# One step of a hybrid attention and state-space encoder on one Trainium2 core: the scan's gate interleaved with the prompt's attention, operand splits moved, preparation reordered

## The reference, cut to what matters

```python
h = rmsnorm(x, g_pre) * (1 + scale) + shift          # shift, scale, gate = split(c @ w_ada + b_ada)
z = h @ w_in                                         # 2048 -> 5712 columns: q, k, v, iq, ik, iw, za, u, zs
# attention group: indexer scores, top-k keys, grouped-query softmax (8 heads, 2 kv heads, 128 wide)
attn = dsa(q, k, v, iq, ik, iw) * silu(za)
# state-space group: 64 groups x 16 channels, 64 complex states each
y = gelu(s5_scan(u))                                 # 1024 columns
y = y * sigmoid(y @ w_glu + b_glu) * silu(zs)        # "the scan's gate"
out = concat([attn, y]) @ w_out                      # 2048 -> 2048
return x + gate * rmsnorm(out, g_post)               # and k, v, ik, last states as outputs
```

## Time and profile before

| | us |
|---|---|
| median of 3 runs | 2370.98 (2365.38 to 2373.74) |
| the profiled execution | 2373.1 |
| its span, first to last instruction | 2371.3 |
| PE busy | 2140.8 (90%) |
| DVE busy | 1268.0 (53%) |
| ACT busy | 718.9 (30%) |
| POOL busy | 355.6 (15%) |
| mean granted clock of TensorE | 0.94 |

### The profile page before, as it was taken

The page is one execution under the profiler, slowest core; times in us unless marked ns, Lnnn a source line. Parts: engine busy times, 40 slices in busy tenths (PEclk is TensorE's granted clock), DMA queues, the critical chain, the costliest instruction groups (busy, mean ns, idle before and its releaser), DMA issues. The chain is left out here.

```text
span 2371.3 us, 33581 instructions
## 1 busy us (share of the span) xinstructions
PE 2140.8 (90%) x12705; PEld 1885.5 (80%) x12705; DVE 1268.0 (53%) x2487; ACT 718.9 (30%) x1433; POOL 355.6 (15%) x614
## 2 busy tenths in 40 slices
PE   5889788899999999999999994978995799998896
PEld 4669788788899999999999994965773578776774
DVE  5446745444324888888776662658764231124224
ACT  5331122211134333333332212336651213321331
POOL 0253652545400000000000000001101100004001
PEclk9999899999999999999999996988997599998997
DMA  9746356555443333333333316232202132227436
GB/s 351 278 164 119 104 127 149 172 172 176 132 117 85 93 95 93 88 93 98 94 90 102 93 52 198 84 117 58 54 1 73 55 90 77 74 71 215 105 93 177
DMA packets 338086, 277.44 MB, mean 117 GB/s; under 512 B 107481, under 2 KB 277409, under 8 KB 336649
## 3 DMA queue, kind: packets, MB, share of 16 engines
q1 hardware_dynamic: 296210, 235.36, 36.1%
q10 hardware_dynamic: 40256, 35.77, 5.0%
q0 software_dynamic: 1472, 4.33, 0.6%
HBM read 215.18 MB, written 60.20 MB: 116 GB/s over the span
## 5 line engine op out<-in xcount | busy, mean ns | idle before, releaser
L1282 PE MATMUL ps_z<-h_hi,w_hi 128*128 128x384 f32 (+2 forms) x1936 | 666.2, 344 | 4.7 <-DVE w_lo L866 4.7
L1284 PE MATMUL ps_z<-h_hi,w_lo 128*128 128x384 f32 (+2 forms) x1936 | 656.9, 339 | 0.0
L1283 PE MATMUL ps_z<-h_lo,w_hi 128*128 128x384 f32 (+2 forms) x1936 | 656.7, 339 | 0.0
L1282 PEld LDWEIGHTS ps_z<-h_hi,w_hi 128*128 128x128 f32 (+1 forms) x1936 | 362.8, 187 | 21.0 <-issue 5.4
L1283 PEld LDWEIGHTS ps_z<-h_lo,w_hi 128*128 128x128 f32 (+1 forms) x1936 | 363.0, 187 | 5.0
L1284 PEld LDWEIGHTS ps_z<-h_hi,w_lo 128*128 128x128 f32 (+1 forms) x1936 | 362.7, 187 | 5.3
L866 DVE TENSOR_TENSOR w_lo<-w_raw,w_hi 128x512 fp32r<-128x512 f32 (+1 forms) x172 | 124.2, 723 | 345.4 <-ACT w_hi L522 343.8
L2644 DVE TENSOR_TENSOR o_lo<-o_raw,o_hi 128x512 fp32r<-128x512 f32 x128 | 90.8, 711 | 293.6 <-ACT o_hi L2606 293.3
L522 ACT ACTIVATE w_hi<-w_raw 128x512 fp32r<-128x512 f32 (+1 forms) x172 | 107.4, 627 | 271.5 <-DMA w_raw<-in_w_in 203.3
L2606 ACT ACTIVATE o_hi<-o_raw 128x512 fp32r<-128x512 f32 x128 | 81.1, 634 | 326.6 <-PE ps_out L2775 260.2
L998 DVE MAX8 top<-score 128x8 f32<-128x1024 f32 (+5 forms) x192 | 171.2, 891 | 3.4
(11 more groups left out here) (428 smaller groups left out, 3289.5 us busy)
## 6 DMA issues: line engine op xcount, KB each, us to landing
w_raw<-in_w_in SPq DMA_DIRECT2D x176, 256.0 KB, 3.1
wada<-in_w_ada SPq DMA_DIRECT2D x32, 1024.0 KB, 9.8
o_raw<-in_w_out SPq DMA_DIRECT2D x128, 256.0 KB
wg<-in_w_ada SPq DMA_DIRECT2D x32, 512.0 KB, 5.0
zt<-z_sb ACTq DMA_DIRECT2D x28, 576.0 KB, 4.2
xs<-in_x_prompt SPq DMA_DIRECT2D x8, 1024.0 KB, 7.9
iq_raw<-zt SPq DMA_DIRECT2D x48, 128.0 KB, 3.3
u<-z_sb ACTq DMA_DIRECT2D x64, 72.0 KB, 3.1
```

The lines of the kernel that those rows point to most:

```text
L1282: M(to, w_hi[q][:, k, 0:m], h_hi[:, kk, cols], start=kk == 0, stop=False)
L1283: M(to, w_hi[q][:, k, 0:m], h_lo[:, kk, cols], start=False, stop=False)
L1284: return M(to, w_lo[q][:, k, 0:m], h_hi[:, kk, cols], start=False, stop=kk == KB - 1)
```

## The change

1. *One program for the scan's gate and the prompt's attention* (`gate_and_attend` in place of `gate_states` and `attend_prompt`). The gate's product is cut into 24 units U (3 slices s of 384 tokens, 8 column blocks i), each of three pieces of 8 matmuls: hi x hi, lo x hi, hi x lo. The 72 pieces are laid evenly over head units 3 to 63. PE's list becomes: turn_rows(n) for n < 9, logits(n+1), the pieces of n, turn(n), values(n-1). y is split by slices, in quarters. `state_tanh`, `glu_tanh`, weights' and values' high parts go into ACT's list, low parts and `mix` into DVE's, and zs * (0.25 tanh + 0.25) * v into POOL's (four operations of 384 columns a unit). turn_rows transposes k, v and the indexer's keys of one tile, beside the attention units 0 to 8; ACT issues their stores. The values for attention come from these transposes instead of from the stored output. ps_o is one bank with two halves, so values(n) waits for the gating of n-1. Early odd gate units use a free half of ps_l[1], the others all ps_g.
2. *Splits at the output projection.* ssm and attention results are kept as plain float32 (`ssm_f`, `attn_f`), also by the decode stage; the first chunk of `project_out` splits row block kb (1152 columns) ahead of the weights' split of kb.
3. *Preparation.* first_products(4p+1) moves into the modulation and first_products(4p+3) behind it; ADA_BUFFER's last eight entries are rotated; the six matrix loads move from ACT's step 9 to SP, after the modulation's loads; turn_c is cut into two, at S = 10 and 12, with two banks; input_matrices and the first output_matrices stand at S = 11, the second at 13; POOL makes three chunks of rotations, DVE five (S = 15 to 19).

```diff
-        ADA_BUFFER = [n % 7 if n < 24 else (n - 24) % 5 for n in range(4 * CHUNKS)]
+        ADA_BUFFER = [n % 7 if n < 24 else (n - 21) % 5 for n in range(4 * CHUNKS)]
...
+            def load_matrices():
+                sp.wait_ge(mod_T, CHUNKS)
...
-                if 16 <= S < 20:
+                if 16 <= S < 21:
                     sp.wait_ge(chunk_ok[1], S - 15)
                     store_chunk(sp, 1, S - 16)
...
-                    if S == 9:
-                        load_matrices()
...
-            for n in range(4):
+            for n in range(3):
                 if n:
                     pool.wait_ge(rot_out[0], 16 * n)
                 rotations(G_, pool, 0, n)
                 store_chunk(pool, 0, n)
...
-                if S == 12:
+                if S == 11:
                     input_matrices()
-                if S == 14:
-                    output_matrices()
+                    output_matrices(0)
+                if S == 13:
+                    output_matrices(1)
                     dve.wait_ge(turn_ok, 1)
-                if 15 <= S < 19:
+                if 15 <= S < 20:
...
+            def turn_c(ri):
                 pe.wait_ge(bc_in, 16 * 6)
+                if ri:
+                    pe.wait_ge(c_read, 1)
...
             for p in range(4):
                 first_products(4 * p)
-                first_products(4 * p + 1)
                 for half in range(2):
                     if p < 3:
                         modulate(2 * p + 2 + half)
-                    first_products(4 * p + 2 + half, (0,))
+                    first_products(4 * p + 1 + half, (0,))
                     if p < 3:
                         turn_modulation(2 * p + 2 + half)
-                    first_products(4 * p + 2 + half, (1,))
+                    first_products(4 * p + 1 + half, (1,))
+                first_products(4 * p + 3)
```

```diff
+    PIECES = (0, 0, 0) + tuple(len(share(3 * GLU, N - 3, n)) for n in range(N - 3))
+    piece_step = [n for n in range(N) for _ in range(PIECES[n])]
+    begins, ends = [piece_step[3 * U] for U in range(GLU)], [piece_step[3 * U + 2] for U in range(GLU)]
+    w_step = [begins[U] - 1 for U in range(GLU)]
+    v_step = [1] + [piece_step[3 * (NB * s - 1) + 1] + 1 for s in range(1, NTC)]
...
+            load_keys(0, 0, FIRST_KEYS)
+            load_q(0)
+            load_values(0, 0, FIRST_KEYS)
+            sp.dma_start(ikT[:], zt[IK0:IW0]).then_inc(ik_in, 16)
+            load_v(0)
+            load_w(0)
+            load_za(0)
+            load_keys(1, FIRST_KEYS, TOK)
+            load_values(1, FIRST_KEYS, TOK)
...
+                G.tensor_tensor(v_sum[:], v_hi[:, i].bitcast(F32), v_lo[s % 2][:, i].bitcast(F32), ALU.add).then_inc(z_step, 1)
+                G.tensor_scalar(half, half, 0.25, 0.25, ALU.mult, ALU.add).then_inc(z_step, 1)
+                G.tensor_tensor(mine, mine, half, ALU.mult).then_inc(z_step, 1)
+                G.tensor_tensor(mine, mine, v_sum[:], ALU.mult).then_inc(zv_ok, 1)
...
+            def value_rows(t):
+                act.wait_ge(kv_T, t + 1)
+                A(v_rows(t), ps_l[0][:, 512 + W:512 + 2 * W], ACT.Copy).then_inc(v_ok, 1)
+                if t >= 2:
+                    act.wait_ge(kv_out[t % 2], 48 * (t // 2))
+                A(ik_rows[:, t % 2], ps_l[0][:, 512:512 + IDX_DIM], ACT.Copy).then_inc(v_ok, 1)
...
+            for n in range(N + 1):
+                if n < N:
+                    exponentials(n)
+                if n < NT:
+                    value_rows(n)
+                for U in range(GLU):
+                    if ends[U] + 1 == n:
+                        glu_tanh(U)
+                if n in v_step:
+                    for quarter in range(QUARTERS):
+                        values_high(v_step.index(n), quarter)
+                if n:
+                    read_turned(n - 1)
+                if 0 <= n - 1 < NT:
+                    store_rows(n - 1)
...
+            for n in range(N + 2):
                 if 1 <= n <= N:
                     normalise(n - 1)
                 if n < N:
                     logits(n)
+                if n < NT:
+                    key_rows(n)
+                if n >= 2:
+                    gate_it(n - 2)
...
+            def glu(p):
+                U, part = divmod(p, 3)
+                if part == 0:
+                    pe.wait_ge(w_hi_ok, U + 1)
+                    earlier = [u for u in range(U) if beside[u] == beside[U]]
+                    if earlier:
+                        pe.wait_ge(g_sig, earlier[-1] + 1)
...
             for n in range(N + 1):
+                if n < NT:
+                    turn_rows(n)
                 if n + 1 < N:
                     logits(n + 1)
                 if n < N:
+                    for p in pieces_at[n]:
+                        glu(p)
                     turn(n)
                 if n:
                     values(n - 1)
```

```diff
+            def mix_high(kb):
+                A(MIX_HI[kb // NB][:, kb % NB], MIX[kb // NB][:, kb % NB], ACT.Copy).then_inc(mix_hi_ok, 1)
...
+            def mix_low(kb):
+                V.tensor_tensor(MIX_LO[part][:, row], MIX[part][:, row], MIX_HI[part][:, row].bitcast(F32), ALU.subtract).then_inc(mix_ok, 1)
```

More of the change, by code:

```diff
@@ L1581, in results, with g_bank @@
+        banks = lambda t: (t + 4) // 4
+        before = [sum(banks(t) for t, _ in units[:n]) for n in range(N + 1)]
+        WIDE = next(n for n in range(N) if banks(units[n][0]) > 1)
+        beside = [U % 2 == 1 and ends[U] + 2 < WIDE for U in range(GLU)]
+        last_beside = max(U for U in range(GLU) if beside[U])
+        def g_bank(U):
+            return ps_l[1][:, 512:512 + TC] if beside[U] else ps_g[:, 0:TC]
         def results(t):
@@ new lines, in load_v, with load_w @@
+            def load_v(s):
+                if s >= 2:
+                    sp.wait_ge(g_pass, 3 * NB * (s - 1))
+                    sp.wait_ge(zv_ok, NB * (s - 1))
+                for half in range(2):
+                    part = slice(NB // 2 * half, NB // 2 * half + NB // 2)
+                    sp.dma_start(v_raw[s % 2][:, part], yv[:, part, s * TC:s * TC + TC]).then_inc(v_in[s][half], 16)
+            def load_w(U):
+                if U >= 3:
+                    sp.wait_ge(g_pass, 3 * (U - 3) + 2)
+                i = U % NB
+                sp.dma_start(w_raw[U % 3][:], wv[:, :, i * P:i * P + P]).then_inc(w_in[U % 3], 16)
@@ L1875, in _ @@
+            for n in range(N):
+                if n == 0:
+                    gates(0)
+                if n % HEADS == 5 and n // HEADS + 1 < TILES:
+                    gates(n // HEADS + 1)
+                for U in range(GLU):
+                    if begins[U] == n:
+                        gated_state(U)
         @block.scalar
@@ L1915, in _ @@
                 if n == 0:
[L1916 removed]
+                    gate_tanh(0)
                 if n % HEADS == 5 and n // HEADS + 1 < TILES:
[L1918 removed]
+                    gate_tanh(n // HEADS + 1)
+                for U in range(GLU):
+                    if begins[U] == n:
+                        state_tanh(U)
         @block.vector
@@ L1965, in _ @@
                     logits(n)
-                if n >= 4:
-                    low(n - 4)
-                if 3 <= n < N + 3:
-                    gate_it(n - 3)
+                if n < NT:
+                    key_rows(n)
+                if n >= 2:
+                    gate_it(n - 2)
+                for U in range(GLU):
+                    if ends[U] + 2 == n:
+                        mix(U)
+                for U in range(GLU):
+                    if w_step[U] == n:
+                        weights_low(U)
+                if n in v_step:
+                    for quarter in range(QUARTERS):
+                        values_low(v_step.index(n), quarter)
         @block.tensor
@@ L2167, in _ @@
             keys(0)
-            for b in range(DEC_B + 2):
+            for b in range(DEC_B + 1):
                 if b + 1 < DEC_B:
@@ L2392, in project_out @@
     ident, gpost, sel = keep["ident"], keep["gpost"], keep["sel"]
-    MIX_HI, MIX_LO = (keep["attn_hi"], keep["ssm_hi"]), (keep["attn_lo"], keep["ssm_lo"])
+    MIX, MIX_HI, MIX_LO = ([keep[n + part] for n in ("attn", "ssm")] for part in ("_f", "_hi", "_lo"))
     NB = KB // 2
```

601 lines of the change are left out of this document (253 added, 348 removed).

## The result

The changed kernel takes 2355.2 us in the median of its runs (2348.9 to 2358.9) against 2369.4 of the kernel before: a ratio of 0.9942, 95% interval 0.9926 to 0.9958. It is 14 us, 0.6%, faster. 2320 was predicted, so less than a third of the forecast gain arrived, and the time lies 3 us outside the range. The profiled execution took 2358.9 us, its span is 2357.1.

The account below looks back on a forecast made before the run. TensorE, busy 90% of the span, was taken as the bound, with its idle and half-clock stretches to gain. From 2373.1: preparation -17, gate and attention -34, output projection +0.7, decode -0.7, giving 2322; as median 2320, range 2293 to 2352.

Parts of the forecast that it names:

- (a): Preparation: first products behind the modulation cover its chain at three quarters and spare slow matmuls, -13.9 us (-9 to -15).
- (b): Preparation: matrix loads moved from ACT to SP save 5.9 us; block 2's weights landing later costs +3 (0 to +6).
- (c): Preparation: turn_c's second half, before quarter S=12, waits for Vector's reading of the first: 7 us new wait (0 to 9).
- (d): Preparation: rotations three on GpSimd, five on Vector; first table's transposes at 259.7 instead of 276.6, making -17 in all.
- Tiles 2 to 7 by the formula: Gate and attention: a unit of tile t takes 0.546 (t+1) + 1.64 + 0.15 us of TensorE; 230 in all.
- Units 2 to 8, 5.0 each for the stores' landing: Gate and attention: units that turn rows wait for the landing of ACT's three stores; +35 us (26 to 41).
- Changes of slice, 3 each: Gate and attention: at two slice changes ACT copies four quarters ahead of read_turned, 3 us each.
- Shared access, 3 us in the terms: Gate and attention: 96 GpSimd operations, 73 us, hold Vector; 0 to 15 us on the path early, 3 counted.
- B: Rival, chance 0.17: ACT and Vector bind the early half; row units 5.8, tiles 1 to 3 +23 us: 2349.
- A: Rival, chance 0.20: TensorE's floor is reached; attention stage -51, preparation -24: 2296 us.
- C: Rival, chance 0.13: preparation gives nothing, as turn_c's wait and Vector's fifth rotation keep the first table's time: 2337 us.
- D: Rival, chance 0.05: slower, as GpSimd's 96 operations each stop Vector between exponential and scaling; 51 us, two thirds, on the path.

Follow-up runs that it names:

- experiment 1: The kernel before with only the changed preparation (`project_in`): 2356.2 us against 2367.1 for the kernel before, ratio 0.996.
- Experiment 3: The changed kernel with Vector's low parts of the gate weights a unit later, behind the scaling: 2318.8 us, ratio 0.9786 to the kernel before.
- Experiment 2: The changed kernel with Vector's low parts of the later slices split two behind each of the next two scalings: 2347.1 us, ratio 0.9909.
- 11: The changed kernel with the weights' low parts a unit later and no splits for the second and third slice: 2307.5 us, ratio 0.9739.
- experiment 7: The changed kernel with weights' and all slices' low parts behind the scaling, and ACT's first attention-gate tanh one unit later: 2313.2 us, ratio 0.9763.
- experiment 4: The changed kernel without GpSimd's four operations a gate unit (96 in all): 2340.7 us, ratio 0.9888.
- experiments 2 to 12: The eleven follow-up variants of the changed kernel, with other list orders, rotation shares or omitted work: 2305.5 to 2347.1 us.
- experiment 5: Both moves: the changed kernel with the weights' low parts a unit later and the later slices' low parts behind the next two scalings: 2308.2 us, ratio 0.9742.

## Why the prediction was right or wrong

*The preparation, -17: right, -14.2.* (a) The quarters' waits, as the earlier trace rows had them, are gone, to 0 and twice 0.4 as worked out; at 107.9 a load of the modulation's weights is late instead, 2.97 us, which I had not seen. So the stretch from the first product to the first of block 2 went from 104.2 to 94.9 us, by 9.3 and not by 13.9. (b) The wait of 4.37 us is gone, and TensorE shows no wait for block 2 that would answer to the +3. (c) The new wait for `c_read` was put at 7 us and is 6.78. (d) The first table was put at 259.7 and comes at 265.6, 5.9 us later. The rows of after, TensorE:

```profile
107.92 5.32 PE L1346 MATMUL ps_w<-wada,cT 128*32 128x512 f32 x26 [2.97 <-DMA wada<-in_w_ada]
120.98 0.45 PE L1306 MATMUL ps_z<-h_hi,w_hi 128*128 128x384 f32 x1 [0.39 <-DVE h_lo L874]
...
195.37 1.09 PE L1361 MATMUL ps_s<-ident,crow 128*128 128x128 f32 x4 [6.78 <-DVEq L1168]
...
265.58 1.76 PE L1371 MATMUL ps_s<-ident,pmat 128*128 128x128 f32 x7 [10.17 <-POOL pmat L804]
```

GpSimd had waited 26.9 us for the last rotation store, which SP issued at 251.3 and not, as I had it, at 243.4: Vector's chunks wait behind its splits of the weights, for which ACT's copies come at TensorE's pace. The table is thus 11.0 us earlier; the other 3.2 came behind it, 2.2 of them at the first wait for `wmat` (4.54 to 2.30 us). That part was not in the sum. Nor does the end hang on the table alone: in experiment 1 the table comes at 262.2, 14.4 earlier, the wait for `wmat` is 4.51 again, and the wait for the batch behind it ends at 341.9 there and at 341.4 here. (Timelines of SP's queue and of GpSimd.)

```profile
251.31 0.34 SPq L329 DMA_DIRECT2D rot<-rot_chunk  x1
```

```profile
255.09 1.69 POOL L791 MEMSET taps<- 16x1920 f32 x1 [26.86 <-DMA rot<-rot_chunk]
```

*Gate and attention, -34: wrong, +1.6.* The step that failed is the price of Vector's new passes: "a mix and the value splits add 0.9" in tile 1, and "Tiles 2 to 7 by the formula", which has no term for them, on the ground that "Tile 7's chain logits to turned, about 5 us, has 7.3 us of other TensorE work beside it". It took Vector's and ACT's new passes as busy time that fits into idle time. But they stand at fixed places in in-order lists, and the weight split stands between the exponential and the scaling. In unit 20, of tile 2, the way from the end of the logits (1521.2) to the scaled probabilities (1527.7) takes 6.5 us, and TensorE is out of other work after 5.8 (1527.1). Of the 37.6 us between 318 and 355.6, units 9 to 15 have 7, the units of tiles 2 to 5 without a change of slice 10, the two changes of slice 12, the end of tile 7 4.4 and the start 3.5. Only in tiles 6 and 7 did the formula hold (45.1 against 44.9; a unit of tile 7 took 5.9 where it says 6.16). Experiment 3 shows that it was that step: with that one place changed the stage takes 316.6, where the sum said 318. I read that agreement with care, since some terms are off in opposite directions in it:
- *Units 2 to 8, 5.0 each for the stores' landing:* 34.9 against 35, but for the wrong reason. With the weights moved they take 24.2, 3.5 each, with the stores still there. The stores don't bind; the split did. So the agreement of the term was luck.
- *Changes of slice, 3 each:* I priced ACT's copies alone. Vector's 3.6 us and the weight's chain stood in line behind them: units 23 and 43, each with one piece, lost 9.8 and 8.2 us beside the formula, 12 more than put. Experiment 2 gave 8 of it back, and in the profile of 11 another 5 go. The waits for the tanh in units 36 and 41, put at 1.7 each, were 1.2 and 1.5.
- *The end of tile 7* took 4.4 more than the 51.3 put, in every version: from the last unit's maximum pass to the next stage it is 14.3 us, with no later unit's work beside its chain, and my tail of 2 was too short.
- *Start, +21 to unit 2:* 24.5. The loads were in by 20.1, as put; the rest is Vector's and ACT's order (a wait of 12.2 us for scaled probabilities): with another order, in experiment 7, the transposes of unit 2 begin at 20.8.

*Shared access, 3 us in the terms:* the 96 operations took 88 us and not 73. Measured: 12 us of longer Vector passes and 15 of time in the kernel after, and 3 (by the profiled stages 5.5) once the queue was put right. The rule of an exclusive lock that lasts a whole instruction (the Trainium skill, "SBUF — State Buffer", "SBUF: two separate sides") agrees with the pair in the earlier trace rows and with the longest mix, 2.63 us where the median is 0.54, which ends behind a multiplication of GpSimd that began just before it:

```profile
L1886 DVE SCALAR_TENSOR_TENSOR ssm_f<-g_tanh,zs x24: 531/544/2630, 1472.0 to 1773.4; 128x384 f32<-128x384 f32 x24
```

```profile
1532.11 2.37 POOL L1719 TENSOR_TENSOR gate<-gate,za 128x1024 f32<-128x1024 f32 x1
1532.26 2.63 DVE L1886 SCALAR_TENSOR_TENSOR ssm_f<-g_tanh,zs 128x384 f32<-128x384 f32 x1
```

That multiplication makes the gate of a tile and is not one of the 96; without them (experiment 4) the longest mix takes 2.63 us too. And most passes never meet GpSimd's: 15 of the 24 mixes take 0.55 us or less.

*Output projection, +0.7:* from its first matmul to that of the second the first chunk takes 64.5 instead of 62.1 us, and 62.9 to 64.8 in the eleven kernels of experiments 2 to 12 with the splits there, in the median 63.2, about +1. *Decode stage, -0.7:* 4 shorter, but 3 of it also in experiment 1, where its code is that of before; so it is no effect of the change.

*The rivals.* B came nearest: 2349, at 0.17. Its sentence, "each extra pass sits in the queue ahead of the next scaling", is what happened, though not its row units; its 23 us in tiles 1 to 3 are 21 by the table, a good part of them at the change of slice, which it doesn't name. I gave it too little because I looked at how busy Vector and ACT were in the earlier trace rows and not at which instruction each new one stands ahead of. A's floor of 2296 was not reached by any version; both moves come within 12 us of it. C, no gain from the preparation, is excluded by experiment 1. D's hold is real, but cost 3 to 15 us and not 51.

## What to carry to other kernels

When work is merged into a stage that is bound by a chain through several in-order lists, cost each new pass by what it stands ahead of, not by its share of an idle engine: a subtraction of 1.2 us, on an engine that was idle 47% of the stage, cost 1.6 us each of 24 times because it stood between the exponential and the scaling. Put passes whose result is needed a step later directly behind the chain's own instruction on that engine, and test the order of the lists before the idea is given up: the merged program was worth nothing as listed, 36 us with one loop moved and 47 with two.

## What was not expected of the hardware

A short wait can cost more than itself. TensorE's busy time for the same matmuls was 288.5 us with 54 us of waits for probabilities and 279.4 with 24. One piece of 8 matmuls took 3.23 us at a granted clock of 0.52, behind a wait of 1.97, and in experiment 5 another took 3.29 behind 2.69, where 1.85 is usual. Not every such wait does it: one of 1.96 us that ended at 1498.7 in the kernel after was followed by a granted clock of 1.00 (1500.0 to 1506.5). The shorter busy time was 9 of the 39 us that the weights' move gave back.

GpSimd's hold was much the same in both orders of Vector's list, 12 and 16 us of longer passes, and cost 15 us in the one and 3 to 5.5 in the other.
